# A gated-DeltaNet and forgetting-attention trunk: two row buffers for queries and keys, and the convolution of a tile ahead of the scaling of the one before it

## The reference

```python
h = rms_norm(x, pre_gain) * (1 + scale) + shift
proj = h @ w_in                                   # 3072 channels of q, k, v, then 1024 of z, then 16 gates
qkv = silu(depthwise_conv(qkv, conv_w))           # 4 taps, causal, along the sequence
q = l2_norm(q by head); k = l2_norm(k by head)    # x * rsqrt(sum(x*x) + 1e-6), 8 heads of 128
# q, k, v then go into the chunked gated delta rule
```

## Time and profile before

| | us |
|---|---|
| median of 3 runs | 3232.22 |
| lowest, highest | 3225.42, 3233.79 |
| the profiled execution | 3229.01 |
| its span in the profile | 3227.2 |
| PE busy | 3048.1 (94%) |
| DVE busy | 1739.5 (54%) |
| ACT busy | 1234.2 (38%) |
| POOL busy | 1018.6 (32%) |
| mean granted clock of TensorE | 0.979 |

### The profile page before, as it was taken

One profiled execution on the slowest core, in us unless ns is written; L12 is line 12 of the kernel. 1 busy time (PEld: TensorE's weight loads), 2 busy tenths in 40 slices (PEclk: granted clock), 3 DMA queues, 4 the chain that ended last, 5 costly groups with the idle time before them and its releaser, 6 DMA issues.

```text
span 3227.2 us, 39990 instructions
## 1 busy us (share of the span) xinstructions
PE 3048.1 (94%) x15148; PEld 2293.9 (71%) x15148; DVE 1739.5 (54%) x2715; ACT 1234.2 (38%) x2161; POOL 1018.6 (32%) x692
## 2 busy tenths in 40 slices
PE   5999989999996999799999999999999999999998
PEld 3766767888885888688887888887555555555587
DVE  4555645567644566565422221103877777777643
ACT  4254455544422455343322211220444444445411
POOL 0497980123224554100000000001455545545400
PEclk8999999999997999899999999999999999999999
DMA  5243341567555666456643432117463423331343
GB/s 223 63 128 118 115 126 55 159 211 224 177 179 163 216 226 204 131 182 199 180 125 105 124 100 78 72 46 170 96 137 90 119 73 98 96 89 47 96 140 124
DMA packets 291068, 428.05 MB, mean 133 GB/s; under 512 B 74638, under 2 KB 187926, under 8 KB 285740
## 3 DMA queue, kind: packets, MB, share of 16 engines
q1 hardware_dynamic: 261596, 359.19, 37.5%
q0 software_dynamic: 13168, 50.42, 4.9%
q10 hardware_dynamic: 16112, 15.86, 1.7%
HBM read 274.58 MB, written 150.69 MB: 132 GB/s over the span
## 4 chain that ended last, share of the span: by engine, by line
PE 53%; ACTq 1%; DVE 1%; issue 1%; ACT 1%; SPq 1%; DMA 1%; POOL 0%; DVEq 0%; POOLq 0%
PE at_ps L1860 7%; PE at_ps L1911 6%; PE at_ps L1763 5%; PE at_ps L1898 5%; PE at_ps L1764 5%; PE at_ps L1765 5%; PE at_ps L1842 4%; PE at_ps L1845 4%; PE at_ps L1828 3%; PE at_ps L1776 2%; PE at_ps L1777 2%; PE at_ps L1778 2%; ACTq L2363 1%; PE at_ps L1874 1%; ACT at_probs L2460 1%
## 5 line engine op out<-in xcount | busy, mean ns | idle before, releaser
L2460 ACT ACTIVATE at_probs<-at_ps 128x512 f32<-128x512 f32 (+3 forms) x640 | 331.4, 534 | 338.4 <-PE at_ps L1845 273.3
L2084 DVE TENSOR_REDUCE at_partial<-at_ps 128x1 f32<-128x512 f32 (+3 forms) x640 | 370.9, 605 | 140.3 <-PE at_ps L1828 107.9
L106 PE MATMUL pa_y<-pa_h_high,pa_w_high 128*128 128x512 f32 x1056 | 422.6, 400 | 12.8 <-ACT pa_acc L772 7.1
L107 PE MATMUL pa_y<-pa_h_low,pa_w_high 128*128 128x512 f32 x1056 | 413.4, 391 | 0.0
L108 PE MATMUL pa_y<-pa_h_high,pa_w_low 128*128 128x512 f32 x1056 | 413.3, 391 | 0.0
L1540 POOL TENSOR_TENSOR at_plain<-at_plain,at_probs 128x512 f32<-128x512 f32 (+3 forms) x256 | 309.5, 1209 | 225.3 <-ACT at_probs L2460 209.4
L1763 PE MATMUL at_ps<-at_h_high,at_w_high 128*128 128x512 f32 x768 | 300.0, 391 | 1.0 <-DVE at_w_low L2013 0.9
L1765 PE MATMUL at_ps<-at_h_high,at_w_low 128*128 128x512 f32 x768 | 299.2, 390 | 0.0
L1764 PE MATMUL at_ps<-at_h_low,at_w_high 128*128 128x512 f32 x768 | 299.1, 389 | 0.0
L1842 PE MATMUL at_ps<-at_h_low,at_h_high 67*128 67x512 f32 (+3 forms) x640 | 260.7, 407 | 12.3 <-ACT at_probs L2460 12.1
L1845 PE MATMUL at_ps<-at_h_low,at_h_high 128*128 128x512 f32 (+3 forms) x640 | 252.9, 395 | 0.0
(11 more groups left out here) (338 smaller groups left out, 5362.0 us busy)
## 6 DMA issues: line engine op xcount, KB each, us to landing
at_h_low<-s_Q SPq DMA_DIRECT2D x96, 256.0 KB, 7.0
s_qkv<-pa_sil POOLq DMA_DIRECT2D x16, 1024.0 KB, 6.6
pa_sil<-s_qkv SPq DMA_DIRECT2D x16, 1024.0 KB, 6.4
dr_kv<-s_qkv SPq DMA_DIRECT2D x16, 1024.0 KB, 8.6
s_Q<-at_parts SPq DMA_DIRECT2D x64, 256.0 KB, 4.1
at_h_high<-s_K SPq DMA_DIRECT2D x32, 512.0 KB, 5.6
pa_wraw<-in_a_w_in_dram ACTq DMA_DIRECT2D x15, 1024.0 KB, 6.0
pa_gb<-in_b_mod_w_dram SPq DMA_DIRECT2D x24, 512.0 KB, 3.6
```

Source lines behind the costliest of these rows:

```text
L106: nc.tensor.matmul(out, w_high[:, k], h_high[:, k], start=k == 0, stop=False)
L107: nc.tensor.matmul(out, w_high[:, k], h_low[:, k], start=False, stop=False)
L2084: reduced.done(v.tensor_reduce(partial[:, u % 2, h * NQ + sub, grp:grp + 1], rough[:, j % 3, 0:width], AX.X, ALU.max))
L2460: probs_ok.done(a.activation(probs[:, R % 2, t, h, off:BLK], logits[:, l % 3, off:BLK], ACT.Exp))
```

## The change

The tiles of queries and keys alternate between two row buffers, `rows = [acc, sil]`. Even tiles are convolved into `acc`, get their SiLU in place, are squared from there, scaled there and stored from there; odd tiles do all this in `sil`. The semaphore `stored` becomes two, one for each buffer. ACT's wait for the store of tile T-1 ahead of the SiLU goes. In its place DVE waits, ahead of the convolution of tile T, for the store of tile T-2. DVE's wait for the SiLU of tile T-1 ahead of the convolution stays for value tiles only. On DVE the convolution of tile T and the scaling of tile T-1 change places. Tile 16, the first of values, is convolved into `acc`, behind the store of tile 14.

```diff
+        rows = [acc, sil]
-        stored, late_stored = st.pool_sem("stored"), st.pool_sem("late_stored")
+        stored, late_stored = [st.pool_sem(f"stored{s}") for s in range(2)], st.pool_sem("late_stored")
...
-            sp.wait_ge(stored, 16 * QK)
+            for s in range(2):
+                sp.wait_ge(stored[s], 16 * QK // 2)
             load_qk(0)
...
                 scaled.wait(pool, T)
-                pool.dma_start(s_qkv[:, :, T].rearrange("c p j -> p c j"), chunk_major(sil[:, :])).then_inc(stored, 16)
+                pool.dma_start(s_qkv[:, :, T].rearrange("c p j -> p c j"), chunk_major(rows[T % 2][:, :])).then_inc(stored[T % 2], 16)
...
             def convolve(T):
-                if T:
+                to = rows[T % 2] if T < QK else acc
+                if T >= QK:
                     silu_done.wait(dve, T - 1)
+                if 2 <= T <= QK:
+                    dve.wait_ge(stored[T % 2], 16 * (T // 2))
...
-                        steps.did(v.tensor_scalar(acc[:, :], x, w, None, ALU.mult))
+                        steps.did(v.tensor_scalar(to[:, :], x, w, None, ALU.mult))
                         continue
                     steps.wait()
-                    ins = v.scalar_tensor_tensor(acc[:, :], x, w, acc[:, :], ALU.mult, ALU.add)
+                    ins = v.scalar_tensor_tensor(to[:, :], x, w, to[:, :], ALU.mult, ALU.add)
...
             def scale(T):
                 rooted.wait(dve, T)
-                scaled.done(v.tensor_tensor(sil[:, :], sil[:, :], sq[:, :], ALU.mult))
+                scaled.done(v.tensor_tensor(rows[T % 2][:, :], rows[T % 2][:, :], sq[:, :], ALU.mult))
...
                         split_next(T)
-                        if 1 <= T <= QK:
-                            scale(T - 1)
                         if kind(T) != "z":
                             bank_free.wait(dve, T, n)
                             convolve(T)
+                        if 1 <= T <= QK:
+                            scale(T - 1)
...
                     if T < QK:
-                        if T:
-                            act.wait_ge(stored, 16 * T)
-                        silu_done.done(a.activation(sil[:, :], acc[:, :], ACT.Silu))
+                        row = rows[T % 2][:, :]
+                        silu_done.done(a.activation(row, row, ACT.Silu))
                         silu_done.wait(act, T)
                         scaled.wait(act, T - 1)
-                        squared.done(a.activation(sq[:, :], sil[:, :], ACT.Square))
+                        squared.done(a.activation(sq[:, :], row, ACT.Square))
```

More of the change, by code:

```diff
@@ L736, in decays @@
                     act.wait_ge(nn_ok, 1)
-                    act.wait_ge(stored, 16 * QK)
+                    for t in range(2):
+                        act.wait_ge(stored[t], 16 * QK // 2)
                 pt_ok.wait(act, c - 1, 1)
```

## The result

The changed kernel takes 3246.2 us (median of 15 runs, 3238.4 to 3271.3) beside 3233.6 us for the one before (15 runs, 3223.9 to 3248.0) on the same chip. The ratio is 1.0052, with a 95% interval of 1.0038 to 1.0066: about 17 us slower (the medians lie 12.6 us apart, the profiled executions 17.9). The forecast was 3234 us, no change. The time lies in the range of 3213 to 3252, but its centre, no change, did not come. What came is close to the slower rival: its pair of tiles was to take 65.0 us and took 64.8, its time was to be 3249. The step of the prediction that came out too small is "the convolution moves ahead of the scaling, and so beside POOL's work". Its direction was right.

The account below looks back on a forecast made before the run. Before, a loop through POOL, store, ACT and PE bound a pair at 60.5 us; after, POOL at 62.0. Tile 16's last bank comes 1.5 us later: 3232.2 + 1.5 gives 3233.7, forecast 3234 us, range 3213 to 3252 for 8 in 10.

Parts of the forecast that it names:

- no change: Whole kernel: within 0.3%, 9.7 us, of before; a pair of 59.8 to 63.6 us; chance 0.53, own range 3223 to 3242.
- slower rival: POOL and DVE hinder each other through the whole pair; payment 7.3 us, pair 65.0 us, kernel 3249 us; chance 0.27.
- the convolution moves ahead of the scaling, and so beside POOL's work: DVE, tile pairs: both convolutions, not one, run beside POOL's terms and lengthen them; 4.3 us more a pair.
- What bounds the kernel before: Query and key tiles: one loop through POOL, the store, ACT and PE, read as 59.4 us of the 60.5 a pair.
- ACT's wait goes, PE's stall moves: 7.0 us of store landing and 5.06 of PE's stall leave the loop; PE waits some 7 us at the modulation sum instead.
- second payment: POOL's loss to scaling and convolution beside it, now for the pair's other tile too: 4.3 us, bounds 0 and 10.7.
- POOL's wait for the even scaling: POOL, before the even tile's store, waits for DVE's scaling: up to 1.2 us a pair, taken as 0.6.
- DVE's chain: From POOL's last addition through sum, banks, split, convolution and scaling: 34.5 us; the odd tile's is hidden by at least 2.6.
- The clock: PE's modulation sum behind the stall runs at half clock, 3.8 us instead of 1.88; POOL clears 4.1 us after its last addition.
- Sum of a pair: Loop of a tile pair: 53.0 + 4.3 + 4.1 + 0.6 = 62.0 us, against 60.5 before.
- The new wait of DVE for the store of T-2: DVE, ahead of the convolution: costs nothing, even store landed at 40.9 us, convolution at 44.9 or later, 4 us to spare.
- Start and end: First clearing at 190.0 instead of 188.52; 7.5 us gained at ACT's gates, tiles 15 to 16; last bank of tile 16 at 586.9.

Follow-up runs that it names:

- half_taps_before: The kernel before with two of the four convolution taps left out in tiles 0 to 11: ratio 0.9978, median 3225.6 us, pair 60.1 us.
- two_buffers: The changed kernel with DVE's old order put back, scaling ahead of convolution, two row buffers kept: ratio 0.9981, median 3226.5 us, pair 58.0 us.
- hybrid: The changed kernel with DVE's old order up to tile 12 and the new one from tile 13: ratio 0.9963, median 3218.5 us, pair 59.5 us.
- light_before: The kernel before without POOL's multiplications of the modulation terms: ratio 1.0016, median 3234.6 us, pair 60.0 us.
- act_before: The kernel before with POOL's multiplications moved to ACT: ratio 1.0033, median 3239.3 us, pair 60.9 us.
- half_taps_after: The changed kernel with two of the four convolution taps left out in tiles 0 to 11: ratio 0.9957, median 3219.4 us, pair 59.5 us.
- light_after: The changed kernel without POOL's multiplications of the modulation terms: ratio 0.9865, median 3185.8 us, pair 53.8 us.

## Why the prediction came out as it did

*What bounds the kernel before.* Right, and half of it. The loop through POOL, store, ACT and PE is there (half_taps_before). That a second one, root to scaling to convolution to square, stood right beside it, at 58.0 to 59.5 us (two_buffers, hybrid), was not seen. The change removes both, so the oversight did not cost the forecast anything; it cost the expectations of light_before and act_before.

*ACT's wait goes, PE's stall moves.* Right: no stall at the square, five at the sum. The forecast had some 7 us for each; they are 7.0 to 14.5, since POOL is later.

*The convolution beside POOL.* The direction was right and the size too small. The second payment was put at 4.3 us, the loss of one tile of before. It is 5.2 us over four pairs by the grouped lines, and 6.3 in the second half of the pair shown. No term in the earlier trace rows is longer than 5.12 us. In two of the new pairs POOL's last multiplication takes 7.00 instead of 2.83: it starts at 436.63 under the last tap, the scaling follows at 438.72 and ends at 441.0, and only then is there the time of a multiplication left. The upper bound, 10.7, was not reached: POOL is kept out for a part of DVE's time only. That this is DVE's work and not the second buffer is shown by half_taps_after, which wins 5.3 us, and by two_buffers.

*POOL's wait for the even scaling.* Taken at 0.6 us with 1.2 as its end; it was 0, 2.45, 2.44, 2.45, and 4.65 in the fifth pair. DVE's chain came out close: from POOL's last addition at 380.48 to the scaling's end at 415.67 it is 35.2 us, against 34.5. The scaling takes 4.5 instead of 2.7, beside POOL. POOL was ready at 33.0. The odd store, held to be hidden by 2.6 us, waited once in the four pairs, 2.45 us, and once before them, 7.04 us. That was not free: where the clearing follows such a late store at once, POOL then waits 3.4 us for the bias, and 1.8 and 1.5 us in the other two pairs.

*The clock.* Right: 3.46 to 3.57 us for the sum where 3.8 was taken, and 3.7 from the last addition to the clearing where 4.1 was forecast. The windows of that stretch, as in the earlier trace rows, with a granted clock of 0.54 and then 1.00:

```profile
380.53:384.00 3.47, 3.47 (x5) 0.41 (x5) 0.00 (x0) 0.00 (x0) 1.12 (x1) 0.54 0.65 196
384.00:385.00 1.00, 1.00 (x5) 0.83 (x6) 0.00 (x0) 0.97 (x1) 0.94 (x1) 1.00 1.02 401
```

*Sum of a pair.* 62.0 forecast, 64.8 measured. Of the 2.8, the payment has 0.9, the even wait 1.2 (7.34 / 4 - 0.6), the odd wait 0.6; less 0.4 for the clock and 0.6 for the pair in which the odd wait already covered PE's sum. Some 1.1 is left. It is the bias wait: 2.5 us in the mean of the four pairs, where the pair from which the 53.0 was added up had 1.3.

*The new wait of DVE for the store of T-2.* Held to cost nothing. It shows three times, 2.2 us at most:

```profile
231.11 1.29 DVE L572 TENSOR_SCALAR pa_acc<-pa_ybuf,pa_taps 128x2048 f32<-128x2048 f32 x1 [2.24 <-DMA s_qkv<-pa_acc]
298.81 2.76 DVE L572 TENSOR_SCALAR pa_acc<-pa_ybuf,pa_taps 128x2048 f32<-128x2048 f32 x1 [0.73 <-DMA s_qkv<-pa_acc]
```

The store of an even tile takes 9.0 us to land by its median, where 7.0 was taken; that of an odd one takes 6.3. No run takes this wait away, so what it costs by itself stays open.

*Start and end.* First clearing 190.7 (190.0 forecast). The gates gave their 7.5 us, as forecast. The last bank of tile 16 was forecast at 586.9 and came 16.4 us later: 0.7 from the start, 11.0 from four pairs, 5.0 from the fifth, -0.4 behind it.

*The rivals.* The slower one was described as it came: DVE and POOL stretched through the pair, POOL waiting for the scaling. It had a chance of 0.27. It was to decide from a payment of 6 us, or from the odd chain passing 66. Neither is how it decided: 5.2 us of payment sufficed, with the waits for the even scaling and for the bias. That its 65.0 us a pair lies so near the 64.8 measured is luck, since it was added up from a payment of 7.3. Payment and even wait grow together, since the meeting of DVE and POOL lengthens POOL's terms and also the scaling for which POOL then waits; to let only one of them grow counts the cause once.

*Still open:* the share of the slow clock, and of DVE's wait for the store.

## What to carry to other kernels

Before a wait is taken away, add up what the next engine does in one turn, and add to it what the moved instructions do to it when they run beside it; a loop of 60 us that gives way to an engine with 53 us of work has 7 us of room, and here a neighbour whose instructions slow its own took all of it and 4 us more. Price that at each place where the two queues meet, and let the neighbour's waits grow with it. If a change frees one chain and loses to another, try the lightening of the other together with it before dropping it: here the change alone made the kernel 17 us slower and the move of the multiplications alone 11 us slower, and both together made it 50 us faster.

## What was not expected of the hardware

Leaving out POOL's multiplications made DVE's convolution longer. Beside multiplications and additions in turn it takes 12.1 us (399.19 to 411.25 in the changed kernel), beside additions alone 15.4:

```profile
332.44 1.28 DVE L565 TENSOR_SCALAR pa_acc<-pa_ybuf,pa_taps 128x2048 f32<-128x2048 f32 x1
333.75 14.11 DVE L568 SCALAR_TENSOR_TENSOR pa_acc<-pa_ybuf,pa_taps,pa_acc 128x2048 f32<-128x2048 f32 x3
```

Three taps that take 7.13 us alone take 14.11 here, 7.0 more, about as much as three undisturbed additions of 2.4 us; POOL runs four between 334.50 and 350.07. Where three taps meet a single addition and no multiplication, they take 2.0 us more (light_after):

```profile
359.46 9.13 DVE L573 SCALAR_TENSOR_TENSOR pa_sil<-pa_ybuf,pa_taps,pa_sil 128x2048 f32<-128x2048 f32 x3
```

The simplest reading is that an addition, with its two inputs from SBUF, costs a tap nearly its whole length, and a multiplication much less: in the earlier trace rows three taps meet one whole addition and one whole multiplication, with the ends of two more terms, and take 9.88, only 2.75 more. The Trainium skill (SBUF — State Buffer, section "Who interferes with whom") says that a DVE instruction with two SBUF inputs and a GpSimd instruction that reads SBUF exclude each other. For the additions this trace agrees. By the rule a multiplication, which reads SBUF too, would cost a tap as much, and that the rows do not show.

In the first half of a pair, 29 us long, POOL gained nothing from two taps fewer: with half the taps three of its terms took 4.05, 3.67 and 4.88 us, and 4.06, 3.66 and 4.88 with all. What POOL pays depends here on which DVE instructions its own meet, not on DVE's time beside it.
